# A hybrid decoder layer on one core: the last down matrices, the residual and the skewed bias table come in pieces, and some sums and splits stand elsewhere

## The reference

```python
def swiglu(x, w_gate, w_up, w_down):
    return (jax.nn.silu(x @ w_gate) * (x @ w_up)) @ w_down

def hybrid_layer(x, ...):
    h = x + 0.5 * swiglu(rms_norm(x, ffn1_norm), ffn1_w_gate, ffn1_w_up, ffn1_w_down)
    u = rms_norm(h, mix_norm)
    z = u @ w_in + b_in
    ...
    ya = dilated_attention(heads(aq), heads(ak), heads(av), rel_bias)
    yb = sliding_window_sink_attention(heads(bq), heads(bk), heads(bv), sinks, rel_bias)
    merged = jax.nn.sigmoid(ga) * (ya @ w_branch_a) + jax.nn.sigmoid(gb) * (yb @ w_branch_b)
    h = h + merged @ w_out
    h = h + 0.5 * swiglu(rms_norm(h, ffn2_norm), ffn2_w_gate, ffn2_w_up, ffn2_w_down)
    return h
```

## Time and profile before

| | us |
|---|---|
| median of 3 runs (lowest, highest) | 2182.69 (2180.88, 2188.42) |
| the profiled execution's own time | 2182.65 |
| its span, first to last instruction | 2180.8 |
| PE busy | 2069.2 (95%) |
| DVE busy | 1395.9 (64%) |
| ACT busy | 787.5 (36%) |
| mean granted TensorE clock | 0.977 of full speed |

### The profile page before, as it was taken

How to read it: one execution, slowest core, us unless ns; L and a number is a source line. 1 busy time by engine, 2 the same in 40 slices (tenths; PEclk the granted TensorE clock), 3 DMA queues, 4 the chain that set the end, 5 groups by cost and what they waited for, 6 DMA issues and landing times. The chain is left out here.

```text
span 2180.8 us, 26744 instructions
## 1 busy us (share of the span) xinstructions
PE 2069.2 (95%) x9564; PEld 1695.4 (78%) x9564; DVE 1395.9 (64%) x2335; ACT 787.5 (36%) x1469; POOL 165.1 (8%) x141
## 2 busy tenths in 40 slices
PE   4899999999999999999999999997899999999996
PEld 2688888887887788888788888885688888877885
DVE  5876766665897534455783444448866666656886
ACT  4433233334455243433562222124423333334453
POOL 3000000000022000032330000001000000000032
PEclk8899999999999999999999999998999999999998
DMA  3232223258335101001002111121223233276333
GB/s 130 73 116 89 105 102 111 97 185 292 97 120 186 53 30 42 37 30 33 16 20 107 49 58 48 48 75 70 93 101 116 102 107 107 78 258 225 97 102 107
DMA packets 81164, 213.23 MB, mean 98 GB/s; under 512 B 8779, under 2 KB 8815, under 8 KB 79888
## 3 DMA queue, kind: packets, MB, share of 16 engines
q1 hardware_dynamic: 69568, 164.66, 22.6%
q10 hardware_dynamic: 10528, 44.06, 5.5%
q0 software_dynamic: 944, 2.88, 0.4%
HBM read 158.58 MB, written 52.98 MB: 97 GB/s over the span
## 5 line engine op out<-in xcount | busy, mean ns | idle before, releaser
L1675 PE MATMUL bank<-T_h,op_h 128*128 128x512 f32 x704 | 276.4, 393 | 15.5 <-ACT s L873 15.5
L1676 PE MATMUL bank<-T_l,op_h 128*128 128x512 f32 x704 | 276.0, 392 | 0.0
L1677 PE MATMUL bank<-T_h,op_l 128*128 128x512 f32 x704 | 275.6, 391 | 0.0
L1675 PE MATMUL bank<-gs_h,op_h 128*128 128x512 f32 x616 | 243.7, 396 | 17.4 <-DVE gs_l L1172 17.4
L1631 PE MATMUL bank<-xh,wh 128*128 128x512 f32 x640 | 255.8, 400 | 0.0
L1633 PE MATMUL bank<-xh,wl 128*128 128x512 f32 x640 | 250.0, 391 | 0.0
L1632 PE MATMUL bank<-xl,wh 128*128 128x512 f32 x640 | 249.9, 390 | 0.0
L1675 PE MATMUL bank<-B_h,op_h 128*128 128x512 f32 x528 | 210.7, 399 | 38.0 <-DVE B_l L1161 21.5
L1677 PE MATMUL bank<-gs_h,op_l 128*128 128x512 f32 x616 | 242.0, 393 | 0.0
L1676 PE MATMUL bank<-gs_l,op_h 128*128 128x512 f32 x616 | 242.0, 393 | 0.0
L1676 PE MATMUL bank<-B_l,op_h 128*128 128x512 f32 x528 | 208.9, 396 | 0.0
(11 more groups left out here) (171 smaller groups left out, 3504.7 us busy)
## 6 DMA issues: line engine op xcount, KB each, us to landing
gr<-g_ops SPq DMA_DIRECT2D x154, 256.0 KB, 2.7
raw<-stream SPq DMA_DIRECT2D x56, 512.0 KB, 3.5
gate<-ffn_in SPq DMA_DIRECT2D x44, 512.0 KB, 4.0
up<-ffn_in SPq DMA_DIRECT2D x44, 512.0 KB, 4.9
g_ops<-tT SPq DMA_DIRECT2D x88, 256.0 KB, 2.0
g_ops<-gb SPq DMA_DIRECT2D x66, 256.0 KB, 5.0
A<-ffn_down ACTq DMA_DIRECT2D x6, 2816.0 KB, 11.1
h_spill<-h ACTq DMA_DIRECT2D x32, 256.0 KB, 2.5
```

Source lines behind the costliest of these rows:

```text
L1675: nc.tensor.matmul(out, op_h[slot][:, cols], hi, start=first, stop=False, skip_group_check=True)
L1676: nc.tensor.matmul(out, op_h[slot][:, cols], lo, start=False, stop=False, skip_group_check=True)
L1677: return nc.tensor.matmul(out, op_l[slot][:, cols], hi, start=False, stop=last, skip_group_check=True)
```

## The change

- A12, A22 and A21 are loaded in two pieces each, slices 0 to 5 (1536 KB) and 6 to 10 (1280 KB). Issue steps, counted from the start of the down stage (step 154): before A12 with the last P4 step of the first stage, A22 at +2, A21 at +4; after A12 first piece as before, its second at +4, A22 at +9 and +14, A21 at +12 and +17. A11 is as before.
- The residual's three DMAs are issued at +10, +24 and +32 instead of all at +8, and DVE waits for each of them at iterations 172, 186 and 198 (before: 172 and, for both others, 176).
- `combine` of T4 and the splits of T3, T4, B22 stand two iterations later (6, 7, 8 instead of 4, 5, 6). `combine` of T3 stays at 3.
- `down_sum` for P3 runs in iterations 189 to 199 instead of 199 to 209.
- `skew` is loaded in four pieces of 640 KB (5 heads), each waiting for two more steps of DVE's splits; `flip`'s second instruction (L702) and the later adds of squares on POOL stand behind the fourth.

```diff
--- before.py
+++ after.py
@@ -397,8 +397,8 @@
         spilled_2 = [sem("spilled_20"), sem("spilled_21")]
         gate_in = [sem(f"gate_in{n}") for n in range(3)]
         up_in = [sem(f"up_in{n}") for n in range(2)]
-        down_in = {x: sem(f"down_in_{x}") for x in ("A11", "A11b", "A21", "A12", "A22")}
-        res_in = [sem("res_in0"), sem("res_in1")]
+        down_in = {x: sem(f"down_in_{x}") for x in ("A11", "A11b", "A12", "A12b", "A22", "A22b", "A21", "A21b")}
+        res_in = [sem(f"res_in{n}") for n in range(3)]
         gr_in = [sem(f"gr_in{n}") for n in range(G_RAW)]
         gw = {x: sem(f"gw_{x}") for x in G_OPS}
 
@@ -696,8 +696,10 @@
             add_squares(1, 0)
             pool.wait_ge(op_low, GROUP_END["P5"])
             nc.gpsimd.memset(flip[:], 0.0).then_inc(flip_made, 1)
-            pool.dma_start(skew[:], bass.AP(tensor=bias_rows.tensor, offset=bias_rows.offset,
-                                            ap=[[1, P], [VEC, HEADS], [1, 2 * P]])).then_inc(skew_in, 16)
+            for n in range(4):
+                pool.wait_ge(op_low, GROUP_END["P5"] + 2 * n)
+                pool.dma_start(skew[:, 5 * n:5 * n + 5, :], bass.AP(tensor=bias_rows.tensor, offset=bias_rows.offset + 5 * n * VEC,
+                                                                    ap=[[1, P], [VEC, 5], [1, 2 * P]])).then_inc(skew_in, 16)
             pool.wait_ge(flip_made, 1)
             nc.gpsimd.affine_select(out=flip[:], in_=flip[:], compare_op=ALU.not_equal, fill=1.0,
                                     base=1 - P, pattern=[[1, P]], channel_multiplier=1).then_inc(flip_made, 1)
@@ -836,7 +838,7 @@
                     n, m = divmod(s - A_STEPS, DEPTH)
                     x = GROUPS[n]
                     if x in ("P1", "P2", "P4"):
-                        block_in = {"P1": "A11" if m < 8 else "A11b", "P2": "A12", "P4": "A22"}[x]
+                        block_in = {"P1": ("A11", "A11b")[m >= 8], "P2": ("A12", "A12b")[m >= 6], "P4": ("A22", "A22b")[m >= 6]}[x]
                         act.wait_ge(down_in[block_in], 16 * (f + 1))
                     else:
                         act.wait_ge(s_made[x], S_MADE * f + FT + m + 1)
@@ -900,8 +902,8 @@
                         gated_high(f, j - A_STEPS + G_LEAD)
                     if j == 0:
                         root_of(2 * f, 1)
-                    if j in (1, 2, 4, 5, 6):
-                        moving_high(f, {1: "T1", 2: "T2", 4: "T3", 5: "T4", 6: "B22"}[j])
+                    if j in (1, 2, 6, 7, 8):
+                        moving_high(f, {1: "T1", 2: "T2", 6: "T3", 7: "T4", 8: "B22"}[j])
 
                     down = [ffn_down[f, b].rearrange("p (m n) -> p m n", n=HALF) for b in range(4)]
                     if j == AT[(FT - 1, "P1")] + 1:
@@ -912,22 +914,30 @@
                         fetch(f, "A11b", A11[:, 8:, :], down[0][:, 8:, :])
                     if j == AT[(FT - 1, "P4")] + 1:
                         act.wait_ge(step_done, base + j)
-                        fetch(f, "A12", A12[:], down[1])
-                    if j == A_STEPS + 2:
+                        fetch(f, "A12", A12[:, 0:6, :], down[1][:, 0:6, :])
+                    if j == A_STEPS + 4:
                         act.wait_ge(step_done, base + A_STEPS)
-                        fetch(f, "A22", A22[:], down[3])
-                    if j == A_STEPS + 4:
-                        fetch(f, "A21", A21[:], down[2])
-                    if j == A_STEPS + 8:
+                        fetch(f, "A12b", A12[:, 6:, :], down[1][:, 6:, :])
+                    if j == A_STEPS + 9:
+                        fetch(f, "A22", A22[:, 0:6, :], down[3][:, 0:6, :])
+                    if j == A_STEPS + 12:
+                        fetch(f, "A21", A21[:, 0:6, :], down[2][:, 0:6, :])
+                    if j == A_STEPS + 14:
+                        fetch(f, "A22b", A22[:, 6:, :], down[3][:, 6:, :])
+                    if j == A_STEPS + 17:
+                        fetch(f, "A21b", A21[:, 6:, :], down[2][:, 6:, :])
+                    src = h_spill if f else xT.rearrange("(k p) t -> p k t", p=P)
+                    if j == A_STEPS + 10:
                         for x in G_OPS:
                             act.wait_ge(gw[x], 16 * DEPTH * (f + 1))
                         if f:
                             for hf in range(2):
                                 act.wait_ge(spilled_2[hf], 16 * KT)
-                        src = h_spill if f else xT.rearrange("(k p) t -> p k t", p=P)
                         act.dma_start(h[:, 0:4, 0:HALF], src[:, 0:4, 0:HALF]).then_inc(res_in[0], 16)
+                    if j == A_STEPS + 24:
                         act.dma_start(h[:, 4:, 0:HALF], src[:, 4:, 0:HALF]).then_inc(res_in[1], 16)
-                        act.dma_start(h[:, :, HALF:], src[:, :, HALF:]).then_inc(res_in[1], 16)
+                    if j == A_STEPS + 32:
+                        act.dma_start(h[:, :, HALF:], src[:, :, HALF:]).then_inc(res_in[2], 16)
                     if j == GROUP_END["P1"]:
                         act.wait_ge(u3_done, pairs + FT)
                         act.wait_ge(g_done[0], pairs + FT)
@@ -1194,7 +1204,7 @@
 
                 made_before = S_MADE * f + FT + m
                 if x == "P5":
-                    dve.wait_ge(down_in["A21"], 16 * (f + 1))
+                    dve.wait_ge(down_in[("A21", "A21b")[m >= 6]], 16 * (f + 1))
                     dve.wait_ge(op_low, STEPS * f + GROUP_END["P2"] + m + 1)
                     out, a, b, op = A22, A21, A22, ALU.add
                 elif x == "P6":
@@ -1362,15 +1372,15 @@
                     if j == 3:
                         for part in range(2):
                             combine(f, "T3", part)
-                    if j == 4:
+                    if j == 6:
                         for part in range(2):
                             moving_low(f, "T3", part)
                         for part in range(2):
                             combine(f, "T4", part)
-                    if j == 5:
+                    if j == 7:
                         for part in range(2):
                             moving_low(f, "T4", part)
-                    if j == 6:
+                    if j == 8:
                         for part in range(2):
                             moving_low(f, "B22", part)
                     if 3 <= j <= A_STEPS + 2 and PAIRS[j - 3][1] == "P3":
@@ -1382,7 +1392,7 @@
                         if n <= j <= A_STEPS + n - 1 and PAIRS[j - n][1] == "P3" and PAIRS[j - n][0] % 2:
                             gated_sum(f, x, PAIRS[j - n][0] // 2)
 
-                    for first, x in ((172, "P5"), (177, "P6"), (188, "P7"), (199, "P3")):
+                    for first, x in ((172, "P5"), (177, "P6"), (188, "P7"), (189, "P3")):
                         if first <= j < first + DEPTH:
                             down_sum(f, x, j - first)
                     if 172 <= j <= 175:
@@ -1390,8 +1400,10 @@
                             dve.wait_ge(res_in[0], 16 * (f + 1))
                         dve.wait_ge(ub_high, 4 * f + j - 171)
                         add_stored(f, 0, j - 172, j - 172)
-                    if j == 176:
-                        dve.wait_ge(res_in[1], 32 * (f + 1))
+                    if j == 186:
+                        dve.wait_ge(res_in[1], 16 * (f + 1))
+                    if j == 198:
+                        dve.wait_ge(res_in[2], 16 * (f + 1))
                     if 199 <= j <= 202:
                         dve.wait_ge(h_added, H_ADDS * f + 13 + j - 199)
                         add_stored(f, 1, j - 199, j - 199)
@@ -1836,7 +1848,7 @@
                         pe.wait_ge(m_out, in_bank + 1)
                     if e[1] == "bias":
                         if e[2] == 0:
-                            pe.wait_ge(skew_in, 16)
+                            pe.wait_ge(skew_in, 64)
                             pe.wait_ge(flip_made, 2)
                         last = nc.tensor.matmul(bank[misc_bank(m)][:], flip[:], skew[:, 2 * e[2]:2 * e[2] + 2, :].rearrange("p h k -> p (h k)"),
                                                 start=True, stop=True)
```

## The result

| | before | after |
|---|---|---|
| median in us (lowest, highest) | 2185.36 (2180.88, 2188.42), 4 runs | 2163.06 (2158.84, 2164.05), 4 runs |
| the profiled execution, its span | 2182.65, 2180.8 | 2158.84, 2157.0 |
| mean granted TensorE clock | 0.977 | 0.981 |

The ratio is 0.9896, 95% interval 0.9871 to 0.9921: the change gains about 1%, more than the 0.3% that can be told from no change. The forecast was 2158.3 us. The sum was made against one profiled execution, and against the profiled one of after (2158.84) it is 0.5 us off; against the median it is 4.8 us off, inside the range.

A forecast was written before the change was run, and what follows sets the result against it. PE, busy 2069.2 of 2180.8 us, was taken to set the time, so its idling and slow stretches could be won. Gains of 16.7 + 3.3 + 3.9 + 0.5 = 24.4 us from 2182.65 gave 2158.3 us, range 2149 to 2171.

The forecast's parts named there:

- Down matrices: Down stages: loading in pieces removes four PE stops for gated blocks and the slow steps behind them, 16.7 us gained.
- blocks landing within 7 us: Sign that the forecast is right: gated blocks in the first third of each down stage land that fast.
- An ACT wait of up to about 5.7 us is free: Down stages: ACT may wait that long for a gated block without stopping PE (8.98 - 3.30).
- Landings of pieces: Load times estimated by size: 6.8 and 5.9 us for down matrix pieces, 3.5 us for a skew piece.
- P3's sums: End of first layer: sums ten iterations earlier make DVE 3.8 us less late, removing two PE stops, 3.3 us gained.
- Skew: End of first layer: four loads remove a 2.61 us PE stop and slow products behind it, 3.9 us gained.
- Starts: Feed-forward layers' starts: later T3, T4 and B22 gain 0.25 us a layer, 0.5 in all, limited by DVE's list.
- the trace of the first layer's start reads the same: Layer starts: the first layer was taken to match the second, 1460 us earlier, with the same 0.25 us gain.
- Blocks do not starve between pieces: Denies the down-stage rival that pieces hold blocks back, costing 8 us in all: 2166.3 us, chance 0.15.
- PE does not keep its lead at the starts: Denies the rival that PE keeps its lead, 4.65 us more gained at each layer's start: 2149.0 us, chance 0.13.
- Nothing of the contention goes: Rival: blocks are late for another cause, so neither the 16.7 nor the 3.9 us come; 2178.9 us, chance 0.10.
- DVE as the bound: Rival where P3's and P7's sums meet: from 0.82 us per DVE instruction PE stops; 2228.3 us, chance 0.05.

The follow-up runs named there:

- fill_three: The changed kernel with three more DVE subtractions of 0.6 us, into unused tiles, behind each of P3's down sums; 2189.38 us, ratio 1.0011.
- residual_together: The changed kernel with the residual's three loads issued together at +8, ahead of A22's first piece; 2162.45 us, ratio 0.9889.
- pieces_early: The changed kernel with both pieces of each quarter issued together at the old steps and the residual's three loads at +8; 2176.34 us, ratio 0.9961.
- late_splits: t3_early with three DVE instructions moved behind C22 and ACT's split for step 13 behind B22's high parts; 2156.16 us, ratio 0.9856.
- t3_early: The changed kernel with T3's split back at iteration 4 and T4's combine at 5; 2155.49 us, ratio 0.9875.

## Why the prediction held, step by step

- **Down matrices, 16.7 us: the size right (16.8), the reason wrong.** The step that failed is "A block that has to wait for one whole piece comes at most 4.1 us later than its usual 2.7, under the free 5.7", from which I took that the smaller load cures it. Blocks came up to 5.9 us later (8.6 us, 489.19) and, in the second layer, 6.5 (9.2 us, 1935.75), so the sign "blocks landing within 7 us" failed too, and still no PE stop was left. With pieces at the old steps about 15 us are lost again, with whole quarters at the new ones 2.6. It is the distance between the loads, together with the place of each issue in ACT's program behind the very split that is late. Both were in the rows: 500.06 and the issue at 500.08, which I did not set side by side. That 16.7 us went is what removing all four stops gives, whatever removes them, so the size could come out right on a wrong reason: luck in the mechanism, not in the sum. The fixed cost of about 2.0 us in the Trainium skill (DMA: Bandwidth & Descriptors, "Anatomy of one DMA — SWDGE (gpsimd) path") is given for DMAs issued from GpSimd; the down matrices are issued from ACT, and no run here isolates a fixed part.
- **"An ACT wait of up to about 5.7 us is free"** held: 7.30 stopped PE for 1.30, 7.95 for 2.19, 7.42 for 2.04, which gives 6.0, 5.8 and 5.4.
- **Landings of pieces**: 6.8 and 7.2 us against estimates of 6.8 and 5.9, and 5.4 against 3.5 for a skew piece. Single pieces took 5.5 to 9.2 us, and the smaller kind took longer by the median, so beside other traffic no line by size gives them.
- **P3's sums, 3.3 us: mis-sized, 2.4.** "So DVE was 3.2 us late, and the sum after that costs another 0.60, which makes 3.8 us less delay" counted the whole lateness as the sums'. Part of it is not theirs. A DVE row of the changed kernel, beside POOL's adds of 8.61 us from 636.53:

```profile
643.93 1.77 DVE L1182 TENSOR_TENSOR gs_l<-gr,gs_h 128x512 fp32r<-128x512 f32 x1
```

  Counted back from the step whose split is late, DVE begins to empty P7's banks 1.8 us earlier than before, not 3.2 (20.3 us ahead of it, 18.5 before); with the sum behind it that is the 2.4. The instructions beside POOL take 1.8 us in both, and a stop of 0.67 stays.
- **Skew, 3.9 us: right**, 4.2 alone. The four issues take 0.87 to 0.92 us each on POOL, not 1.35.
- **Starts, 0.5 us: right in the second layer, too small in the first.** In the second: P5 4.90 us earlier (4.9 forecast), DVE idle for 0.76, 0.76 and 0.33 (0.8, 0.8, 0.4), U3 16.73 us behind S4, 0.67 more than before (0.6), 0.33 us gained (0.25). In the first layer it is 1.25. That "the trace of the first layer's start reads the same" was the slip: there, before the change, U3 waited 1.35 us for PE (0.51 in the second), and P5 started 45.40 us behind the first product (41.47), so PE and not DVE's list was last and its earlier start was worth more. From P5 to P3 PE took 11.16 us at a mean granted clock of 0.72 there, 10.25 at 0.82 in the second layer; why it was lower is open.
- **The sum**: 16.8 + 2.4 + 4.2 + 1.6 are 25.0 us, and the two layers are 25.0 shorter. The two profiled executions differ by 23.8, since attention and merge took 1.7 more; that the forecast of 24.4 comes within 0.6 of this is in part luck, a term of 0.9 too much and one of 1.1 too little beside a stretch that nobody forecast.
- **The rivals.** Blocks do not starve between pieces, and PE does not keep its lead at the starts. "Nothing of the contention goes" did not come in time, but the contention itself is still there in the landings; what went is its reaching PE. For DVE as the bound I had a threshold of 0.82 us each and gave PE a credit of 5.7 us; fill_three shows a credit of 5.85, and that such a price must also hold the banks' emptying, the eleventh step and the slow products. Its condition did not arise.

## What to carry to other kernels

Look where a load is issued in its engine's program: if it stands behind an instruction that waits for data which the load before holds back, the loads chain themselves, and here moving them apart gave most of the gain while cutting them up alone gave next to none. A stop of PE is worth its length only if no other engine's list sets the end of the phase: read that list from its first row to the row that frees PE, and count its idle time. For terms of 2 us compare marks inside one profile, not medians.

## What was not expected of the hardware

- The same code of attention and merge took 777.2 to 782.3 us, and the tail 18.0 to 19.9, from one profiled execution to another. From PE's first product on, the layers' stretches of the changed kernel agree within 0.2 us (671.6 and 671.7, 656.4 and 656.6), but that is two executions, and a dip of the clock can add more, as the 1.6 us in the second layer of residual_together and of pieces_early.
- Where PE's pauses at a layer's start were made shorter, the slow products did not go away. In late_splits and t3_early the first layer's stretch from P5 to P3 of tile 0 has the same mean clock (0.86 and 0.87) with the slow steps in other places. In the second layer the same stretch took 11.14 us without a pause at 0.73, against 12.72 with 2.39 us of idling at 0.87, so 1.58 of the 2.39 us reached the time.
- A DVE instruction of 0.68 us takes 1.77 to 1.79 beside POOL's additions.
- A block of 256 KB that lands in 2.7 us took 6.2 with the residual's 2 KB rows in flight and 9.7 to 12.2 with the down matrix pieces queued behind it.
